# Neighbourhood attention steps regrouped on TensorE: scores, both heads' transposes, values

## The chip, the cores and the metric

The kernel is one launch on one core of a Trainium2 chip. The metric is the device time of that launch in microseconds; lower is better. A core has five engines that matter here: TensorE (PE, with its weight loads shown as PEld), VectorE (DVE), ScalarE (ACT), GpSimd (POOL) and SyncE (SP, which here issues loads). They run on their own and wait for each other by semaphores.

## What is computed

Two blocks in a row over 1024 positions of width 1024. The first block is two layers; each normalises, projects, runs three kinds of attention (latent, neighbourhood, differential), gates and projects back. The second block is a state space mixer, another attention and two wide feed-forward parts, and takes most of the time. The change touches neighbourhood attention alone, whose core in the reference is:

```python
def neighborhood_attention(q, k, v, rpb, scale):       # 16 rows of 64 columns, 6 heads of 64
    ...
    def one(r):
        r0 = jnp.clip(r - kr // 2, 0, rows - kr)
        q_r = lax.dynamic_index_in_dim(qg, r, axis=1, keepdims=False)
        k_r = lax.dynamic_slice_in_dim(kg, r0, kr, axis=1)[:, :, col_idx]
        v_r = lax.dynamic_slice_in_dim(vg, r0, kr, axis=1)[:, :, col_idx]
        ...
        s = jnp.einsum('bchd,brcjhd->bhcrj', q_r, k_r, preferred_element_type=jnp.float32) * scale
        s = s + bias.transpose(0, 2, 1, 3)[None].astype(jnp.float32)
        p = jax.nn.softmax(s.reshape(B, H, GRID_W, kr * kc), axis=-1).reshape(B, H, GRID_W, kr, kc)
        return jnp.einsum('bhcrj,brcjhd->bchd', p.astype(v.dtype), v_r)
```

## The kernel before

Each layer has a projection stage, then this neighbourhood stage, then a differential and a latent stage. Between stages every engine drains and waits for the other three (`phase_end`), and TensorE runs a few filler products (`keep_busy`) so as not to stand idle.

The neighbourhood stage is 24 steps: 3 pairs of heads (hp) times 8 tiles of 128 queries (t). Step s handles both heads of a pair, units u = 2s and 2s + 1. A query tile sees a window of keys: 512 of them in an outer step (t = 0, 1, 6, 7) and 576 in an inner one (t = 2 to 5, `inner` true), of which 12 exist per layer. The data passes through four engines:

- TensorE `scores(s)` (L1412): both heads' scores, one head in each half of the array's rows, into PSUM banks 0 to 3. It waits until the maxima of the step before are taken (m_ready 2s).
- VectorE `top(u)` (L3151 to L3167): one fused custom operation adds the bias and takes the maximum (L3161), and a small operation negates it (L3166), which raises m_ready. Each third of the stage needs its bias: top(0), top(16) and top(32) first wait for bias_in0 or bias_in1 (L3151).
- ScalarE `exps(u)` (L2247): the exponential with its sum (a second small record, the accumulator read).
- TensorE `probs_t(u)` (L1426): one head's probabilities are transposed in pieces of 128 keys into banks 4 and 5, four for an outer step and five (the last 64 wide) for an inner one.
- ScalarE `evacuate(u)` (L2257) copies the transposed tile to SBUF; for the odd head of an inner step VectorE copies the 64-key rest (`probs_t`, L3173).
- TensorE `values_of(s)` (L1442): the product with the values, both heads side by side in bank 6; an inner step has a last part over 64 rows.
- VectorE `out(s)` (L3178): the copy of the result.

TensorE's order in one pass of the loop is: probs_t(2s - 1), scores(s + 1), probs_t(2s), values_of(s - 1). The transposed buffers are three: one for the odd heads and two for the even.

After 8 steps, a pair's sums are inverted (L3209) and widened by GpSimd into a table that lies over the pair's bias in SBUF (`na_wides`, L623; the table of pair 0 over bias 0). In steps 11, 12, 19 and 20 TensorE transposes halves of such a table (`factors`, L1455, bank 7), and VectorE multiplies the outputs by it (`normed_out`, L3187). VectorE also does ten pieces of a key rotation in steps 10 to 19 (`key_rope`, L2936 to L2944).

The third pair's bias uses the same memory as the first pair's table. Its load is issued by SyncE, in code that the change leaves as it is:

```python
                sp.wait_ge(sems["t_done"], 6 * layer + 2)                                  # L888
                rows = a["na_bias"][layer * 3 + 2].rearrange("p (j n) -> p j n", j=2)
                sp.dma_start(na_bias[0], rows).then_inc(sems["bias_in0"], 16)              # L890
                for rr in range(2):
                    q, first = slice(64 * rr, 64 * rr + 64), (4 + rr) * GW
                    sp.dma_start(na_inner[2][q, :, rr * GW:rr * GW + NA_W], rows[q, :, first:first + NA_W])\
                        .then_inc(sems["bias_in0"], 16)                                    # L893
```

`t_done` rises by one with each factor turn (four in this stage, two in the next), so L888 waits for the second factor turn of the layer.

In the last pass TensorE also issues the first scores of the differential stage (`df_scores`, L1474), VectorE takes their maxima (`maximum`, L2928) and ScalarE the exponentials (`df_exp`, L2265).

## Time and profile before

| | us |
|---|---|
| median of 3 timed runs | 3862.62 |
| lowest of them | 3857.7 |
| the profiled execution | 3865.42 |
| its span, first to last instruction | 3863.6 |

The three timed runs were 3862.62, 3857.7 and one of 12884.99. The mean granted TensorE clock of the profiled execution is 0.995 of full speed. In the profile, "busy" is the time in which an engine has an instruction under way; "idle before" is what it stood before an instruction, with what released it. "issue" there means that no event of another engine is seen that released it.

### The profile page before, as it was taken

How to read it: one execution, taken by the hardware profiler on the slowest of the kernel's cores; microseconds unless marked ns; L12 is line 12 of the kernel's file. 1: busy time of each engine (PE TensorE's matmuls, PEld its weight loads, DVE VectorE, ACT ScalarE, POOL GpSimd, SP SyncE). 2: the span in 40 equal slices, each digit the busy share in tenths (PEclk: the TensorE clock that was granted, in tenths of full speed). 3: DMA queues.
4: the chain of work that ended last, by engine and by line, in shares of the span. 5: the costliest groups of instructions: out<-in, count | busy, mean ns of one | idle time of the engine just before them, and what ended most of it. 6: DMA issues, size and time to landing. Idle time of an engine off the chain costs nothing.

```text
span 3863.6 us, 53821 instructions
## 1 busy us (share of the span) xinstructions
PE 3774.8 (98%) x21662; PEld 2942.4 (76%) x21662; DVE 2660.7 (69%) x3327; ACT 1931.0 (50%) x2848; POOL 659.3 (17%) x747
## 2 busy tenths in 40 slices
PE   8999999999999999999999899999999999999999
PEld 5876667887876667887854668888888888888887
DVE  4446967675346967534445654989889869888898
ACT  5336866324336866324356444444445554444454
POOL 0120121001120121011059921000001430000010
PEclk9999999999999999999999999999999999999999
DMA  5232000453332000331100011111111111111111
GB/s 210 93 96 53 1 1 12 175 210 107 93 96 53 1 1 13 120 117 71 50 16 1 26 44 61 67 59 44 55 66 55 48 41 66 55 44 55 66 55 66
DMA packets 67735, 247.55 MB, mean 64 GB/s; under 512 B 15648, under 2 KB 16288, under 8 KB 55456
## 3 DMA queue, kind: packets, MB, share of 16 engines
q1 hardware_dynamic: 53648, 193.51, 14.9%
q10 hardware_dynamic: 13840, 50.60, 3.5%
q8 instruction: 173, 2.83, 0.3%
q14 instruction: 74, 0.61, 0.0%
HBM read 206.34 MB, written 29.36 MB: 61 GB/s over the span
## 4 chain that ended last, share of the span: by engine, by line
PE 82%; DVE 6%; POOL 4%; ACT 3%; issue 3%; DMA 1%; DVEq 0%; SPq 0%; ACTq 0%; POOLq 0%
PE ps L1786 31%; PE ps L1042 13%; PE ps L1294 3%; PE ps L1296 3%; PE ps L1295 3%; PE ps L1474 2%; PE ps L1157 2%; PE ps L1190 2%; PE ps L1532 2%; PE ps L1521 2%; PE ps L1426 2%; PE ps L1442 1%; PE ps L1412 1%; DMA w<-in_wstream 1%; PE ps L1175 1%
## 5 line engine op out<-in xcount | busy, mean ns | idle before, releaser
L1786 PE MATMUL ps<-x_piece1hi,w_piece1hi 128*128 128x512 f32 x672 | 262.4, 390 | 0.2 <-DVE x_piece1lo L3523 0.2
L1786 PE MATMUL ps<-x_piece0hi,w_piece0hi 128*128 128x512 f32 x672 | 262.3, 390 | 0.0
L1786 PE MATMUL ps<-x_piece0hi,w_piece0lo 128*128 128x512 f32 x672 | 261.5, 389 | 0.0
L1786 PE MATMUL ps<-x_piece1hi,w_piece1lo 128*128 128x512 f32 x672 | 261.4, 389 | 0.0
L1786 PE MATMUL ps<-x_piece0lo,w_piece0hi 128*128 128x512 f32 x672 | 261.4, 389 | 0.0
L1786 PE MATMUL ps<-x_piece1lo,w_piece1hi 128*128 128x512 f32 x672 | 261.4, 389 | 0.0
L1786 PE MATMUL ps<-x_piece2hi,w_piece2lo 128*128 128x512 f32 x672 | 261.4, 389 | 0.0
L1786 PE MATMUL ps<-x_piece2hi,w_piece2hi 128*128 128x512 f32 x672 | 261.4, 389 | 0.0
L1786 PE MATMUL ps<-x_piece2lo,w_piece2hi 128*128 128x512 f32 x672 | 261.4, 389 | 0.0
L1042 PE MATMUL ps<-n_hi_m,w_lo 128*128 128x512 f32 x576 | 225.5, 391 | 0.0
L4045 POOL TENSOR_TENSOR rope_cos<-rope_cos,arena 128x512 f32<-128x512 f32 x42 | 65.4, 1557 | 734.1 <-ACT arena L2497 731.0
L2928 DVE TENSOR_REDUCE small<-ps 128x1 f32<-128x1024 f32 x128 | 154.3, 1212 | 26.8 <-PE ps L1474 26.8
L2989 DVE TENSOR_REDUCE small<-ps 128x1 f32<-128x1024 f32 x96 | 113.0, 1219 | 79.6 <-PE ps L1164 79.4
L2265 ACT ACTIVATE h<-ps,small 128x1024 f32<-128x1024 f32 x128 | 142.6, 1114 | 46.8 <-DVE small L2928 46.7
L4045 POOL TENSOR_TENSOR rope_sin<-rope_sin,arena 128x512 f32<-128x512 f32 x28 | 45.2, 1615 | 640.7 <-ACT arena L2497 638.3
L2551 ACT ACTIVATE m<-m 128x1024 f32<-128x1024 f32 x80 | 85.0, 1062 | 132.5 <-DVE m L3567 104.0
L1786 PEld LDWEIGHTS ps<-x_piece1hi,w_piece1hi 128*128 128x128 f32 x672 | 126.1, 188 | 27.2 <-DVE x_piece1lo L3523 0.6
L1786 PEld LDWEIGHTS ps<-x_piece0lo,w_piece0hi 128*128 128x128 f32 x672 | 126.1, 188 | 26.6 <-issue 0.5
L1786 PEld LDWEIGHTS ps<-x_piece0hi,w_piece0hi 128*128 128x128 f32 x672 | 126.1, 188 | 26.6 <-DVE w_piece1lo L3516 0.2
L1786 PEld LDWEIGHTS ps<-x_piece1lo,w_piece1hi 128*128 128x128 f32 x672 | 126.1, 188 | 26.6 <-issue 0.5
L1786 PEld LDWEIGHTS ps<-x_piece1hi,w_piece1lo 128*128 128x128 f32 x672 | 126.1, 188 | 26.3
L1786 PEld LDWEIGHTS ps<-x_piece0hi,w_piece0lo 128*128 128x128 f32 x672 | 126.1, 188 | 26.2
(514 smaller groups left out, 10722.2 us busy)
## 6 DMA issues: line engine op xcount, KB each, us to landing
w<-in_wstream SPq DMA_DIRECT2D x87, 1024.0 KB, 5.1
arena<-in_wstream SPq DMA_DIRECT2D x40, 1024.0 KB, 4.9
arena<-in_wstream ACTq DMA_DIRECT2D x16, 1024.0 KB, 5.1
n_saved<-n_hi_m SPq DMA_DIRECT2D x16, 512.0 KB, 7.3
n_saved<-n_lo SPq DMA_DIRECT2D x16, 512.0 KB, 8.3
n_hi_h<-n_saved SPq DMA_DIRECT2D x16, 512.0 KB, 8.0
n_lo<-n_saved SPq DMA_DIRECT2D x16, 512.0 KB, 9.0
out<-h ACTq DMA_DIRECT2D x32, 256.0 KB, 2.2
```

Source lines behind the costliest of these rows:

```text
L1042: last = mm(dst, a_part[:, k, wcols], b_part[:, tile0 + k, :], start=(k == 0 and b_part is hi and a_part is wb[0]), stop=(k == nk - 1 and ...
L1157: mm(ps[:, 2 * j + hf, :], lt_split(hp, 0, q, r)[a_part], lt_split(hp, 1, keys, r)[b_part], start=(part == 0), stop=False)
L1190: last = mm(ps[64 * j:64 * j + 64, 6, 0:P], lt_v[:, b, hp * P + 64 * j:hp * P + 64 * j + 64], lt_pt_of(2 * s + j)[:, b * P:b * P + P], sta ...
L1294: mm(dst, wb[0][:, k, wcols], hi[:, k, :], start=(step == 0), stop=False)
L1295: mm(dst, wb[0][:, k, wcols], lo[:, k, :], start=False, stop=False)
L1296: last = mm(dst, wb[1][:, k, wcols], hi[:, k, :], start=False, stop=(step == KT - 1))
L1786: last = mm(dst[:, e, :], a_part[:, pair, k, f], b_part[:, k, :], start=(n in FRESH and half == 0 and k == 0 and t == 0), stop=(half == 1 ...
L2265: nc.scalar.activation(df_p[:, 2 * (c % 3) + i, :], psf[:, 2 * i * HALF:(2 * i + 2) * HALF], ACT.Exp, bias=negm[:, e:e + 1], accum_out=sum ...
L2551: nc.scalar.activation(x, x, ACT.Square if st.kind == "up" else ACT.Sigmoid).then_inc(sems["unit_done"], 1)
L2928: V.reduce_max(negm[:, u:u + 1], src, AX.X, negate=True).then_inc(sems["m_ready"], 1)
L2989: V.reduce_max(negm[:, u:u + 1], psf[:, 2 * j * HALF:(2 * j + 2) * HALF], AX.X, negate=True)\
L4045: G.tensor_tensor(out=x, in0=x, in1=ring[:, r % 2, :], op=ALU.add).then_inc(sems["t_added"], 1)
```

## The change

- TensorE's order in a pass becomes scores(s + 1), probs_t(s), values_of(s - 1). probs_t now takes a step: both heads' transposes in one group. In an inner step the two 64-key rests come first, into bank 5; then four transposes of the even head into bank 4 and four of the odd head into bank 7. t_full rises once for each head.
- Evacuation is by head: ScalarE copies the even head (bank 4) and, in inner steps, both rests; VectorE copies the odd head (bank 7). pt_act and pt_dve now count steps.
- The transposed buffers become two pairs, by the parity of the step; the fourth buffer is new (`na_pt_odd`).
- `top` multiplies by -1.0 and takes a minimum, so the negated maximum comes from the fused operation itself; the exponential takes scale -1.0, and L3166 goes.
- The factor turns go to bank 5 and to steps 14, 15, 22 and 23 (`NA_FACTORS_AT`), after values_of; an inner turn of the next pair that would reuse bank 5 waits for their multiplication.
- The first differential scores and their maxima come one pass earlier, in step 23. At the start the eight filler products stand between scores(1) and the first transposes.

```diff
-NA_INNER_AT = [sum(x[3] for x in NA_PAIRS[:s]) for s in range(NA_STEPS + 1)]
+NA_FACTORS_AT = {NT * (hp + 1) + NT - 2 + hf: (hp, hf) for hp in range(NA_H // 2 - 1) for hf in range(2)}
...
         def na_pt_of(u):
-            return na_pt[:, 1, :] if u % 2 else na_odd[:, 0, :] if u // 2 % 2 else na_pt[:, 0, :]
+            if u // 2 % 2:
+                return na_pt_odd if u % 2 else na_odd[:, 0, :]
+            return na_pt[:, u % 2, :]
...
-                    def probs_t(u):
-                        pe.wait_ge(sems["exp_done"], T.since("exp_done", u + 1))
-                        if u:
-                            pe.wait_ge(sems["pt_act"], T.since("pt_act", u))
-                        if u and u % 2 == 0:
-                            pe.wait_ge(sems["pt_dve"], T.since("pt_dve", NA_INNER_AT[u // 2]))
-                        for b, size in key_tiles(NA_PAIRS[u // 2][3]):
-                            last = nc.tensor.transpose(ps[0:size, 4 + b // 4, (b % 4) * P:(b % 4) * P + P],
-                                                       na_p_of(u)[:, b * P:b * P + size], ident)
-                        last.then_inc(sems["t_full"], 1)
+                    def probs_t(s):
+                        hp, t, _, inner = NA_PAIRS[s]
+                        pe.wait_ge(sems["exp_done"], T.since("exp_done", 2 * s + 2))
+                        if s:
+                            pe.wait_ge(sems["pt_act"], T.since("pt_act", s))
+                        if inner and s - 3 in NA_FACTORS_AT:
+                            pe.wait_ge(sems["na_m_done"], T.since("na_m_done", 2 * hp - 2))
+                        for j in range(2 if inner else 0):
+                            nc.tensor.transpose(ps[0:GW, 5, j * P:j * P + P], na_p_of(2 * s + j)[:, NA_W:NA_INNER], ident)
+                        for j in range(2):
+                            if s and j:
+                                pe.wait_ge(sems["pt_dve"], T.since("pt_dve", s))
+                            for b in range(NA_W // P):
+                                last = nc.tensor.transpose(ps[:, 7 if j else 4, b * P:b * P + P],
+                                                           na_p_of(2 * s + j)[:, b * P:b * P + P], ident)
+                            last.then_inc(sems["t_full"], 1)
...
                     for s in range(NA_STEPS + 1):
-                        if s == NA_STEPS:
+                        if s + 1 < NA_STEPS:
+                            scores(s + 1)
+                        elif s + 1 == NA_STEPS:
                             pe.wait_ge(sems["m_ready"], T.since("m_ready", NA_U))
...
                                 df_scores(0, i)
-                        if s:
-                            probs_t(2 * s - 1)
-                        if s + 1 < NA_STEPS:
-                            scores(s + 1)
-                        if s < NA_STEPS:
-                            probs_t(2 * s)
                         if s == 0:
                             keep_busy(7, 8)
+                        if s < NA_STEPS:
+                            probs_t(s)
                         if s:
                             values_of(s - 1)
-                        if s > NT and s % NT in (3, 4):
-                            factors(s // NT - 1, s % NT - 3)
+                        if s in NA_FACTORS_AT:
+                            factors(*NA_FACTORS_AT[s])
...
-                    def evacuate(u):
-                        act.wait_ge(sems["t_full"], T.since("t_full", u + 1))
-                        if u == 2:
+                    def evacuate(s):
+                        act.wait_ge(sems["t_full"], T.since("t_full", 2 * s + 1))
+                        if s == 1:
                             act.wait_ge(sems["restored"], 2 * 16 * KT * (layer + 1))
-                        if u >= 3:
-                            act.wait_ge(sems["o_full"], T.since("o_full", u // 2 - 1 + u % 2))
-                        width = NA_K if u % 2 == 0 and NA_PAIRS[u // 2][3] else NA_W
-                        nc.scalar.activation(na_pt_of(u)[:, 0:width], psf[:, 4 * HALF:4 * HALF + width], ACT.Copy)\
-                            .then_inc(sems["pt_act"], 1)
+                        if s >= 2:
+                            act.wait_ge(sems["o_full"], T.since("o_full", s - 1))
+                        for j in range(2 if NA_PAIRS[s][3] else 0):
+                            nc.scalar.activation(na_pt_of(2 * s + j)[0:GW, NA_W:NA_K], ps[0:GW, 5, j * P:j * P + P], ACT.Copy)
+                        nc.scalar.activation(na_pt_of(2 * s)[:, 0:NA_W], ps[:, 4, :], ACT.Copy).then_inc(sems["pt_act"], 1)
...
-                    for s in range(NA_STEPS + 1):
-                        if s < NA_STEPS:
-                            exps(2 * s)
-                        if s:
-                            evacuate(2 * s - 1)
-                        if s < NA_STEPS:
-                            exps(2 * s + 1)
-                            evacuate(2 * s)
+                    exps(0)
+                    exps(1)
+                    for s in range(NA_STEPS):
+                        evacuate(s)
+                        if s + 1 < NA_STEPS:
+                            exps(2 * s + 2)
+                            exps(2 * s + 3)
...
-                            na_inner[hp][:, j, :] if inner else na_bias[hp % 2][:, j, e * GW:e * GW + NA_W], 1.0, 4 * MASKED, ALU.add, ALU.max, mx[:, u:u + 1])\
-                            .then_inc(sems["v_link"], 1)
-                        dve.wait_ge(sems["v_link"], T.next("v_link"))
-                        V.tensor_scalar(negm[:, u:u + 1], mx[:, u:u + 1], -1.0, None, ALU.mult)\
+                            na_inner[hp][:, j, :] if inner else na_bias[hp % 2][:, j, e * GW:e * GW + NA_W], -1.0, -4 * MASKED, ALU.add, ALU.min, negm[:, u:u + 1])\
                             .then_inc(sems["m_ready"], 1)
-                    def probs_t(u):
-                        dve.wait_ge(sems["t_full"], T.since("t_full", u + 1))
-                        if u >= 3:
-                            dve.wait_ge(sems["o_full"], T.since("o_full", u // 2 - 1 + u % 2))
-                        V.tensor_copy(na_pt_of(u)[0:GW, NA_W:NA_K], ps[0:GW, 5, 0:NA_K - NA_W]).then_inc(sems["pt_dve"], 1)
+                    def probs_t(s):
+                        dve.wait_ge(sems["t_full"], T.since("t_full", 2 * s + 2))
+                        if s >= 2:
+                            dve.wait_ge(sems["o_full"], T.since("o_full", s - 1))
+                        V.tensor_copy(na_pt_of(2 * s + 1)[:, 0:NA_W], ps[:, 7, :]).then_inc(sems["pt_dve"], 1)
...
                     for s in range(NA_STEPS + 1):
-                        if s == NA_STEPS:
-                            maximum(0, psf[:, 0:2 * HALF], NA_STEPS)
-                        if s and NA_PAIRS[s - 1][3]:
-                            probs_t(2 * s - 1)
-                        if s == NA_STEPS:
-                            maximum(1, psf[:, 2 * HALF:4 * HALF], NA_STEPS)
                         if s + 1 < NA_STEPS:
                             top(2 * s + 2)
                             top(2 * s + 3)
+                        elif s + 1 == NA_STEPS:
+                            for i in range(2):
+                                maximum(i, psf[:, 2 * i * HALF:2 * i * HALF + 2 * HALF], NA_STEPS)
+                        if s < NA_STEPS:
+                            probs_t(s)
                         if s:
                             out(s - 1)
...
-                        if s > NT and s % NT in (3, 4):
-                            normed_out(s // NT - 1, s % NT - 3)
+                        if s in NA_FACTORS_AT:
+                            normed_out(*NA_FACTORS_AT[s])
```

## Rows read from the trace of the kernel before

**Rows 1.** The page: busy time and share of the span by engine

```profile
PE 3774.8 (98%) x21662; PEld 2942.4 (76%) x21662; DVE 2660.7 (69%) x3327; ACT 1931.0 (50%) x2848; POOL 659.3 (17%) x747
```

**Rows 2.** By stretch: length, busy PE, PEld, DVE, ACT, POOL, granted clock, DMA share, GB/s

```profile
265.00:363.50 98.50, 96.30 (x849) 63.68 (x849) 62.38 (x202) 69.51 (x152) 16.63 (x15) 1.00 0.20 57
...
277.00:353.00 76.00, 75.73 (x691) 50.13 (x692) 51.87 (x171) 55.47 (x123) 5.39 (x4) 1.00 0.16 44
```

**Rows 3.** Waits, 275 to 358 us: who for whom, us, times, longest

```profile
PEld ps L1426 <- issue: 12.0, 30, 1.0
...
PEld ps L1412 <- DVE small L3166: 0.7, 4, 0.2
```

**Rows 4.** Timeline (start us, length us), TensorE's weight loads, one inner step

```profile
280.62 0.30 PEld L1412 LDWEIGHTS ps<-arena 64*128 64x128 f32 x4 [0.20 <-issue]
...
281.85 0.50 PEld L1426 LDWEIGHTS ps<-mats,m 128*128 128x128 f32 x5
282.54 0.85 PEld L1442 LDWEIGHTS ps<-h,arena 128*64 128x64 f32 x16 [0.20 <-issue]
...
284.63 0.30 PEld L1412 LDWEIGHTS ps<-arena 64*128 64x128 f32 x4 [0.20 <-issue]
```

**Rows 5.** Timeline, TensorE's products, an outer turn and outer values

```profile
303.84 0.66 PE L1426 MATMUL ps<-mats,m 128*128 128x128 f32 x4
304.43 1.09 PE L1442 MATMUL ps<-h,arena 128*64 128x128 f32 x16
305.45 0.66 PE L1426 MATMUL ps<-mats,m 128*128 128x128 f32 x4
```

**Rows 6.** Timeline, weight loads, a factor turn directly ahead of a turn

```profile
312.99 0.42 PEld L1455 LDWEIGHTS ps<-mats,h 128*128 128x128 f32 x4 [0.17 <-issue]
313.38 0.55 PEld L1426 LDWEIGHTS ps<-mats,m 128*128 128x128 f32 x5
314.12 0.30 PEld L1412 LDWEIGHTS ps<-arena 64*128 64x128 f32 x4 [0.20 <-issue]
```

**Rows 7.** Timeline, ScalarE: an evacuation and an exponential

```profile
280.73 0.60 ACT L2257 ACTIVATE h<-ps 128x512 f32<-128x512 f32 x1 [0.26 <-PE ps L1426]
281.22 0.77 ACT L2247 ACTIVATE m<-m,small 128x576 f32<-128x576 f32 x1
281.89 0.19 ACT L2247 ACTIVATION_READ_ACCUMULATOR m<-m,small 128x1 f32 x1
```

**Rows 8.** Timeline, VectorE's narrow copy

```profile
280.73 0.28 DVE L3173 COPY h<-ps 64x128 f32<-64x128 f32 x1 [0.34 <-PE ps L1426]
```

**Rows 9.** Timeline, VectorE's top(32): the fused operation and its accumulator read

```profile
327.75 0.69 DVE L3161 CUSTOM_DVE_ANT_0 h<-ps,h 128x512 f32<-128x512 f32 x1 [0.96 <-PE ps L1412]
328.37 0.08 DVE L3161 DVE_READ_ACCUMULATOR2_ANT small<- 128x1 f32 x1
```

**Rows 10.** Timelines of VectorE, ScalarE and TensorE at the end of the stage

```profile
359.75 2.35 DVE L2928 TENSOR_REDUCE small<-ps 128x1 f32<-128x1024 f32 x2 [0.59 <-PE ps L1474]
...
363.15 0.19 ACT L2265 ACTIVATION_READ_ACCUMULATOR h<-ps,small 128x1 f32 x1
...
363.49 0.18 PEld L1474 LDWEIGHTS ps<-df_hi 32*128 32x128 f32 x1 [0.45 <-ACT h L2265]
```

**Rows 11.** Timelines of TensorE and load queue; the queue's issues (size, us to landing)

```profile
317.54 0.66 PE L1455 MATMUL ps<-mats,h 128*128 128x128 f32 x4
...
318.23 0.34 SPq L890 DMA_DIRECT2D h<-in_na_bias  x1
318.61 1.22 SPq L893 DMA_DIRECT2D w<-in_na_bias  x2
...
w<-in_na_bias SPq DMA_DIRECT2D x2, 256.0 KB, 6.6
```

**Rows 12.** By stretch, the next stage (columns as in rows 2)

```profile
368.00:371.20 3.20, 0.78 (x7) 0.48 (x6) 3.20 (x3) 1.20 (x2) 0.00 (x0) 1.00 1.04 247
371.20:385.00 13.80, 13.80 (x78) 10.26 (x76) 9.86 (x12) 9.91 (x15) 1.02 (x3) 0.51 0.61 125
```

More of the change, by code:

```diff
@@ L1402, in _ @@
                 phase_end(LAYER_COUNTS.n % 4, 5)
-                with T.span(s_full=NA_STEPS, m_ready=NA_U, exp_done=NA_U, t_full=NA_U, pt_act=NA_U, pt_dve=NA_INNER_AT[-1], o_full=NA_STEPS,
+                with T.span(s_full=NA_STEPS, m_ready=NA_U, exp_done=NA_U, t_full=NA_U, pt_act=NA_STEPS, pt_dve=NA_STEPS, o_full=NA_STEPS,
                             o_free=NA_STEPS, t_done=4, na_m_done=4):
@@ L1417, in key_tiles @@
                         return [(b, P) for b in range(NA_W // P)] + [(NA_W // P, GW)] * inner
-                    def probs_t(u):
-                        pe.wait_ge(sems["exp_done"], T.since("exp_done", u + 1))
-                        if u:
-                            pe.wait_ge(sems["pt_act"], T.since("pt_act", u))
-                        if u and u % 2 == 0:
-                            pe.wait_ge(sems["pt_dve"], T.since("pt_dve", NA_INNER_AT[u // 2]))
-                        for b, size in key_tiles(NA_PAIRS[u // 2][3]):
-                            last = nc.tensor.transpose(ps[0:size, 4 + b // 4, (b % 4) * P:(b % 4) * P + P],
-                                                       na_p_of(u)[:, b * P:b * P + size], ident)
-                        last.then_inc(sems["t_full"], 1)
+                    def probs_t(s):
[14 more added lines that the diff above has]
+                            last.then_inc(sems["t_full"], 1)
                     def values_of(s):
                         hp, t, s0, inner = NA_PAIRS[s]
-                        pe.wait_ge(sems["pt_act"], T.since("pt_act", 2 * s + 2))
-                        pe.wait_ge(sems["pt_dve"], T.since("pt_dve", NA_INNER_AT[s + 1]))
+                        pe.wait_ge(sems["pt_act"], T.since("pt_act", s + 1))
+                        pe.wait_ge(sems["pt_dve"], T.since("pt_dve", s + 1))
                         if s:
@@ L1450, in factors @@
                             pe.wait_ge(sems["na_m_done"], T.since("na_m_done", 2 * hp + hf))
-                        factor_turns(hp, hf, 7)
+                        factor_turns(hp, hf, 5)
                     def factor_turns(hp, hf, bank):
@@ L2237, in _ @@
                 inner_bias(layer, 1, "bias_in1")
-                with T.span(s_full=NA_STEPS, m_ready=NA_U, exp_done=NA_U, t_full=NA_U, pt_act=NA_U, pt_dve=NA_INNER_AT[-1], o_full=NA_STEPS,
+                with T.span(s_full=NA_STEPS, m_ready=NA_U, exp_done=NA_U, t_full=NA_U, pt_act=NA_STEPS, pt_dve=NA_STEPS, o_full=NA_STEPS,
                             o_free=NA_STEPS, t_done=4, na_m_done=4):
@@ L3144, in _ @@
                 phase_end()
-                with T.span(s_full=NA_STEPS, m_ready=NA_U, exp_done=NA_U, t_full=NA_U, pt_act=NA_U, pt_dve=NA_INNER_AT[-1], o_full=NA_STEPS,
+                with T.span(s_full=NA_STEPS, m_ready=NA_U, exp_done=NA_U, t_full=NA_U, pt_act=NA_STEPS, pt_dve=NA_STEPS, o_full=NA_STEPS,
                             o_free=NA_STEPS, t_done=4, na_m_done=4):
@@ L3182, in normed_out @@
                         dve.wait_ge(sems["o_free"], T.since("o_free", NT * (hp + 1)))
-                        out_times(hp, hf, 7)
+                        out_times(hp, hf, 5)
                     def out_times(hp, hf, bank):
```

4 lines of the change are left out of this document (3 added, 1 removed).

## The prediction

> **What bounds the kernel now.** The page comes first: TensorE is busy for 98% of the span [rows 1], mostly on lines of other stages. The edited stage runs once per layer and lasts 98.5 us in the first [rows 2], so some 197 us of 3863.6 for both: whatever happens here moves the whole by tenths of a per cent unless a step breaks. About 2% (77 us) is what a measurement of this kernel tells from no change, and I give my chances by that.
>
> Next, who waits inside the stage. In the 76 us of steady stepping TensorE is busy 75.7 us at the full granted clock (2.4 GHz) [rows 2]. In the list of waits its weight loads wait for "issue", and for another engine next to never: 0.7 us in all for the negated maximum [rows 3]. So the stage goes at TensorE's own pace, and what it pays besides its columns is a gap of some 0.2 us whenever one kind of product follows another. The timeline of one inner step (576 keys) shows it: scores at 280.62, a turn of five transposes from 281.85 to the values at 282.54, then the values and the other head's turn, and scores again at 284.63, 4.01 us later [rows 4]. A turn of five costs 0.69 us from start to start; in outer steps (512 keys) a turn of four costs 0.59 (303.84 to 304.43) and the values 1.02 (304.43 to 305.45) [rows 5].
>
> **The merge of the two turns.** The kernel before holds its own measurement of a merge. At 312.99 four factor transposes stand directly ahead of a turn of five, and the nine end at the scores of 314.12: 1.13 us [rows 6]. Apart they would take 0.59 and 0.69 [rows 4, 5], 1.28. The waits between them (the turn waits on three counts) cost nothing, so a merge saves 0.15 us. One more full transpose is 0.10 to 0.11; ten in one group are then 1.24 instead of 1.39, eight 1.02 instead of 1.17. Steps 2 to 22, 21 of them, give 21 x 0.15 = 3.15 us per layer.
>
> In the new turn the narrow transposes (64 columns) come first, then the full ones. In the turn of five the narrow one follows four full ones and adds only 0.10 us (0.69 against 0.59) [rows 4, 5], so I cost that order at nothing. The Trainium skill, TensorEngine Tiling, section Key Properties, says that changing the tiling mode drains the engine. If narrow and full transposes were two modes, each inner step would pay one change back, an estimate of 12 x 0.15 = 1.8 us per layer; the row shows no such change.
>
> **The four factor turns** lose a part of it. Before they lean on a transpose turn and cost 1.13 - 0.69 = 0.44 us each; after, in steps 14, 15, 22 and 23, they stand between values and scores as a group of their own, 0.59. 4 x 0.15 = 0.6 us lost per layer.
>
> **ScalarE and VectorE, costed at nothing, and by what cover.** ScalarE now has per inner step two narrow copies, one 512 copy and two exponentials, all between one turn and the next. A 512 copy lets the next operation start 0.50 us after it; an exponential ends with its accumulator read 0.86 after its start [rows 7]. For a 64x128 copy on ScalarE there is no row: more than nothing, less than those 0.50; I take the 0.28 of VectorE's copy of that shape [rows 8]. From the start of a turn of ten: 0.91 to the end of its first half, 0.56, 0.50, 0.77 for the first exponential, 0.86 for the second, 0.05 to TensorE: 3.65 us, 3.1 to 4.1 by the bounds. The new period is 4.01 - 0.15 = 3.86. It fits; where it does not, 12 inner steps lose the excess. VectorE loses a negation and takes a 128x512 copy (nearest row: the 0.69 of the fused operation on 512 columns [rows 9]) for its narrow one: 0.8 + 0.8 + 0.7 + 0.3 = 2.6 us per step and up to 0.7 of key rotation, under 3.86. The fused minimum has no row either; it reads and writes what the maximum does, so I take the same 0.69; a third more would still be covered. The removed negation was not on the path [rows 3].
>
> **Start and end.** At the start the second turn waits some 0.5 us for ScalarE, as both exponentials now stand ahead of it, and the group that is gone gives about as much back: an estimated 0.06 us lost. At the end the first differential scores come one pass earlier. The two maxima (2.35 us) then stand ahead of VectorE's last copy, and the last values, waiting for it, come about when they did. But ScalarE's two large exponentials, which were the last thing before the next stage (their read at 363.15 ends 363.34, TensorE follows at 363.49 [rows 10]), are over by then, and VectorE's last reciprocal closes the stage an estimated 0.75 us sooner. Per layer: 3.15 - 0.6 - 0.06 + 0.75 = 3.2 us gained, 6.5 for both.
>
> **What the moved factor turn releases.** The second factor turn does more than feed VectorE: L888 makes the load queue wait for it (t_done at 6*layer + 2) before it loads the third pair's bias. In the trace the turn runs 317.54 to 318.20 and the queue issues at 318.23; the last of its three loads is issued about 1.0 us later and lands 6.6 us after that [rows 11]. So the bias is whole some 7.6 us after the turn. Before, the turn is in step 12 and the bias is first needed by top(32), in step 15, which runs at 327.75, 9.5 us after the issue, and waits for the scores [rows 9]: the load is covered, with 2 us to spare. After, the turn is the last thing that TensorE does in step 15, and top(32) stands first in VectorE's step 15. The cover is gone altogether.
>
> Queued behind top(32) on VectorE are top(33), the copy of the odd head, the output of step 14, the factor multiplication and a key rotation. ScalarE's next exponential waits for top(32); TensorE goes on to the end of the factor turn and stops, since scores(17) need top(33). The load queue has nothing else due. From the turn's end: 7.65 us to the landing, 0.05 to VectorE, 0.8 + 0.75 for the two tops, 0.15 to TensorE = 9.4 us, where the scores would have started at once. The factor turn needs nothing of top(32), so it is a stall and no deadlock. Afterwards VectorE works its queue off and is late for top(34); some 0.5 us of that reaches TensorE.
>
> **Sum.** Per layer 9.4 + 3 - 3.2 = +9.2 us, for both +18.4. The profiled span of 3863.6 becomes 3882. That execution took 3865.42 with what lies around its span, 2.8 over the median of 3862.62; the median should become 3862.62 + 18.4 = 3881.
>
> **Rivals.**
> 1. The bias is there in time, and the kernel is faster than before. For it I find only an error of mine in the order of the steps; against it the queue's issue 0.03 us after the very turn that moves. It decides from a landing before the end of scores(16). 3862.6 - 6.5 = 3856. Chance 0.05.
> 2. The stall as above, but the merge saves nothing: narrow and full transposes drain between them, or ScalarE's chain is at its upper bound (4.1 over 3.86, 12 steps, 2.9 us). At most the 3.15 us of both layers come back: 3887. Chance 0.15.
> 3. Slower by more than 2%: the half clock, once there, stays for the rest of the stage. Steps 17 to 23, about 25 us, would take twice that: 2 x (9.4 + 25 - 3.2) = 62, 3925. It passes 77 us only if 7.5 us more are lost in each next stage. For it: 13.8 us at half clock with TensorE busy [rows 12]; against it: 76 us of the same steps at the full one [rows 2]. Chance 0.03, of which a third over 2%.
>
> **How the numbers follow.** The forecast has 0.77. Its own range comes from the clock: with no loss 2 x (9.9 - 3.2) = 13, 3876; with all of it 2 x (9.4 + 6.9 - 3.2) = 26, 3889. Scatter between executions (3857.7 to 3865.4 before) and rival 2 widen this to 3868 to 3894, which leaves out rivals 1 and 3 and the tails. Within 2% is 3785 to 3940; chances are 0.01 faster, 0.97 within, 0.02 slower.
>
> **What the profile after would show.** One group of eight or ten transposes of 1.02 or 1.24 us per step: the merge. The bias load issued at the end of a factor turn near 328 us, and VectorE idle some 10 us ahead of the fused operation of top(32), released by a load: the stall. A granted clock of 0.5 in a stretch behind it: the clock's part. If TensorE waits for ScalarE in inner steps, that cover was misjudged; if no engine is idle around step 15, the forecast is wrong and rival 1 right.

## The result and the profile after

| | before | after |
|---|---|---|
| median, us | 3862.68 (6 runs) | 3875.06 (6 runs) |
| range of them | 3857.7 to 12884.99 | 3872.04 to 3881.64 |
| the profiled execution | 3865.42 | 3881.47 |
| its span | 3863.6 | 3879.7 |

The kernel became slower by a third of a per cent: the ratio of after to before is 1.0031, with an interval of 1.0021 to 1.0041. The interval leaves out 1, so the rise is clear of the scatter; by the 2% bound of the prediction it counts as no change. The median rose by 12.4 us where 18.4 were forecast, and 3875 lies inside the range given. The ratios here and below are formed without the executions in a disturbed, slow state (the one of 12884.99 and, in the first experiment, one of 3987.44), which the medians and the numbers of runs include.

The page's busy times (busy us, share of the span, instructions):

```profile
PE 3771.7 (97%) x21662; PEld 2946.6 (76%) x21662; DVE 2668.3 (69%) x3255; ACT 1908.9 (49%) x2848; POOL 661.8 (17%) x747
```

Against [rows 1] TensorE has the same 21662 instructions and 3 us less busy time, in a span 16 us longer: it stood idle for more. VectorE has lost 72 instructions net (96 negations and 24 narrow copies gone, 48 wide copies new); ScalarE's number is unchanged. The stretches of the stage say where the idleness is. The columns are length, busy PE, PEld, DVE, ACT and POOL, granted clock, DMA share and GB/s; the first two lines are the stage in both layers, then its steady part, the stall, and two stretches at half clock:

```profile
265.50:370.40 104.90, 94.68 (x849) 65.39 (x848) 65.71 (x166) 57.99 (x152) 17.11 (x16) 0.95 0.19 54
1141.40:1247.00 105.60, 95.26 (x849) 65.83 (x848) 65.71 (x166) 58.00 (x152) 17.08 (x15) 0.95 0.19 53
277.00:327.00 50.00, 50.00 (x482) 34.67 (x480) 33.89 (x88) 32.28 (x88) 4.83 (x4) 1.00 0.14 35
327.00:337.00 10.00, 0.99 (x12) 0.58 (x8) 1.45 (x5) 0.72 (x2) 0.00 (x0) 0.67 0.55 170
330.30:340.60 10.30, 3.69 (x12) 2.07 (x12) 4.42 (x12) 2.05 (x6) 0.00 (x0) 0.50 0.40 135
1212.70:1217.80 5.10, 5.05 (x24) 3.22 (x26) 3.79 (x9) 2.83 (x9) 0.00 (x0) 0.50 0.00 0
```

From the first scores of the stage to the first of the next, the stage took 98.31 us before and takes 104.72 now (265.71 to 370.43); in the second layer it went from 98.3 to 105.5. That is 6.4 + 7.2 = 13.6 us for both, against 12.4 in the medians. The other 2.5 us of the two spans' difference lie outside this stage: 0.5 of them before it begins, the rest behind it, where the two traces have stretches of 3.4 us at half clock in different places (at 514 and 2258 us before, at 879 and 1398 after). No run here explains these. The half clock of the next stage, too, differs between kernels whose code there is the same (13.7 us in each layer before, 3.4 and 13.6 in the first experiment, in one profiled execution of each). The medians carry all of that; the stage's own length does not, and is the safer measure in what follows.

The stall is one place per layer. TensorE's products there (start, length, engine, line, operation, output and inputs, shapes, count, idle before and releaser):

```profile
326.22 1.09 PE L1452 MATMUL ps<-h,arena 128*64 128x128 f32 x16
327.24 0.66 PE L1465 MATMUL ps<-mats,h 128*128 128x128 f32 x4
336.91 2.08 PE L1416 MATMUL ps<-arena 64*128 64x512 f32 x4 [9.01 <-DVE small L3168]
338.92 1.86 PE L1436 MATMUL ps<-mats,h 128*128 128x128 f32 x8
...
341.74 1.30 PE L1416 MATMUL ps<-arena 64*128 64x512 f32 x8
```

The load queue and VectorE in the same stretch, in the same columns:

```profile
327.93 0.34 SPq L894 DMA_DIRECT2D h<-in_na_bias  x1
328.31 1.23 SPq L897 DMA_DIRECT2D w<-in_na_bias  x2
...
324.85 0.68 DVE L2951 TENSOR_TENSOR arena<-arena,h 128x512 f32<-128x512 f32 x1
335.55 0.69 DVE L3168 CUSTOM_DVE_ANT_0 h<-ps,h 128x512 f32<-128x512 f32 x1 [10.02 <-DMA w<-in_na_bias]
```

Read them together. The factor turn (L1465) starts at 327.24. The queue, which had waited for it, issues the bias at 327.93 where before it issued at 318.23 [rows 11]. VectorE has nothing that it may do from 325.53 to 335.55, when the last part of the load releases top(32). TensorE's scores(17) (336.91) wait for top(33). Then the first scores take 2.08 us for what took 1.13 before: that is the half clock.

And the inner step, by TensorE's weight loads:

```profile
281.01 0.30 PEld L1416 LDWEIGHTS ps<-arena 64*128 64x128 f32 x4 [0.17 <-issue]
...
282.23 0.14 PEld L1431 LDWEIGHTS ps<-mats,m 128*64 128x64 f32 x2
282.37 0.91 PEld L1436 LDWEIGHTS ps<-mats,m 128*128 128x128 f32 x8
283.45 0.85 PEld L1452 LDWEIGHTS ps<-h,arena 128*64 128x64 f32 x16 [0.17 <-issue]
284.47 0.20 PEld L1452 LDWEIGHTS ps<-h,arena 64*64 64x64 f32 x4 [0.17 <-issue]
284.84 0.30 PEld L1416 LDWEIGHTS ps<-arena 64*128 64x128 f32 x4 [0.17 <-issue]
```

Scores to scores is 3.83 us (281.01 to 284.84), where [rows 4] had 4.01. The narrow transposes run 282.23 to 282.37 and the full ones follow without a gap. The group of ten takes 1.22 us to the values. All of TensorE's 50 us in 277 to 327 are busy.

The account of the first layer, in differences between the starts of scores (scores(23) is the last; "next" is the first of the next stage):

| stretch | before | after | difference |
|---|---|---|---|
| first scores to scores(3) | 11.77 | 11.83 | +0.06 |
| scores(3) to scores(16) | 49.39 | 46.59 | -2.80 |
| scores(16) to scores(17), the stall | 3.25 | 12.78 | +9.53 |
| scores(17) to scores(18), half clock | 3.26 | 4.83 | +1.57 |
| scores(18) to scores(23) | 19.86 | 18.06 | -1.80 |
| scores(23) to next | 10.78 | 10.63 | -0.15 |
| sum | 98.31 | 104.72 | +6.41 |

So the regrouping does what it should, and the moved factor turn takes back more than that. The runs below take the pieces apart.

### The profile page after: what moved, and what is told of

Same layout as the page of the kernel before. It is cut to its first block, busy times and chain, and to the rows that moved or that the text cites. A ratio compares the mean times of both kernels' runs of the same rounds, so it can differ in the third digit from the quotient of the medians.

```text
span 3879.7 us, 53675 instructions
## 1 busy us (share of the span) xinstructions
PE 3771.7 (97%) x21662; PEld 2946.6 (76%) x21662; DVE 2668.3 (69%) x3255; ACT 1908.9 (49%) x2848; POOL 661.8 (17%) x747
## 4 chain that ended last, share of the span: by engine, by line
PE 56%; DVE 5%; POOL 3%; ACT 2%; issue 2%; DVEq 0%; ACTq 0%; POOLq 0%
PE ps L1794 31%; PE ps L1046 4%; PE ps L1298 2%; PE ps L1299 1%; PE ps L1300 1%; PE ps L1484 1%; PE ps L1584 1%; PE ps L1161 1%; PE ps L1194 1%; PE ps L1540 1%; PE ps L1529 1%; PE ps L1736 1%; PE ps L1734 1%; PE ps L1735 1%; PE ps L1752 1%
```

## The experiments

**The load's dependency removed, all else kept.** The theory: the loss is entirely the bias load that waits for the moved factor turn. So give it a reason to come early. The third pair's bias could not be loaded because the first pair's table lay in its memory; here that table goes to memory that is free in the stage, and the load waits only for the first pair's sums to be inverted, at which its scores no longer need bias 0.

```diff
+        na_wide0 = [region(w[hf], 2 * NA_INNER, NT // 2, P)[0] for hf in range(2)]
...
-                sp.wait_ge(sems["t_done"], 6 * layer + 2)
+                sp.wait_ge(sems["lat_rs"], 2 * LAT_PAIRS * layer + 1)
...
+                            wide = na_wides[hp][:, 4 * hf + i, :] if hp else na_wide0[hf][:, i, :]
+                            last = nc.tensor.transpose(ps[:, bank, i * P:i * P + P], wide, ident)
...
```

The part left out has GpSimd write the table's two halves to the new place.

> The changed kernel, with the first pair's table put into free columns of w[0] and w[1] instead of over bias 0, so that the load of the third pair's bias no longer waits for the second factor turn; it waits for the first pair's reciprocal (step 8). Factor turns stay in steps 14, 15, 22, 23. If the late load causes the stall, the 9.0 and 9.1 us idle stretches ahead of scores(17) and the half clock behind them are gone: from scores(16) to scores(18) the changed kernel takes 17.6 us against 6.8 without a stall, so 2 x 10.8 = 21.6 us less than 3875.1, 3853.5 us, 9 us under the kernel before. Rival: the stall is only part and the regrouping itself gains nothing; then it cannot come under 3862.7 us. Rival: the idle stretch has another cause (bank 5, the multiplication); then 3875 stays.

Measured: 3854.33 us (11 runs), ratio 0.9978 (0.9969 to 0.9987). The queue, VectorE's top(32) and TensorE around the place where the stall was:

```profile
302.43 0.34 SPq L895 DMA_DIRECT2D h<-in_na_bias  x1
...
325.38 0.69 DVE L3170 CUSTOM_DVE_ANT_0 h<-ps,h 128x512 f32<-128x512 f32 x1
...
323.95 1.13 PE L1417 MATMUL ps<-arena 64*128 64x512 f32 x4
...
327.64 1.13 PE L1417 MATMUL ps<-arena 64*128 64x512 f32 x4
...
330.75 1.30 PE L1417 MATMUL ps<-arena 64*128 64x512 f32 x8
```

The load goes out 25 us earlier, top(32) no longer waits for it, and the steps are 3.69 and 3.11 us where after had 12.78 and 4.83. The stage takes 93.93 us, 10.8 less than in after and 4.4 less than before; over two layers the latter is 8.8. The median is 8.7 us under that of before in the same set of runs (3862.99). The theory holds, and the regrouping is worth 4.4 us per layer, more than the 3.2 forecast.

**The factor turns alone moved in the kernel before.** The other direction: if the moved turn makes the loss, it makes it without any regrouping.

```diff
-                        if s > NT and s % NT in (3, 4):
-                            factors(s // NT - 1, s % NT - 3)
+                        if s in NA_FACTORS_AT:
+                            factors(*NA_FACTORS_AT[s])
...
```

VectorE's multiplication by the factors moves in the same way.

> The kernel before, with one part of the change alone: the factor turns and their multiplications in steps 14, 15, 22, 23 instead of 11, 12, 19, 20. If the place of the second factor turn makes the stall, it appears here too: about 9 us idle and 1.5 to 2.5 us of slow clock per layer, some 21 us in all, 3883 us. If the stall needs the new grouping (the third bank, the copies by head), this stays at 3862.7 us within 1 us.

Measured: 3888.51 us (5 runs), ratio 1.0065 (1.0053 to 1.0077). Around the stall, TensorE:

```profile
327.77 0.66 PE L1456 MATMUL ps<-mats,h 128*128 128x128 f32 x4
...
337.89 2.08 PE L1413 MATMUL ps<-arena 64*128 64x512 f32 x4 [9.03 <-DVE small L3167]
```

The same 9.0 us (9.28 in the second layer) with the old groups. The stage is 109.6 us long, 11.3 more than before. Two layers of that are 22.6 us, of the 25.5 by which the median lies over before's (3862.99), so some 3 us lie outside this stage. Inside it, the half clock lasted into the steps after the stall: scores(17) to scores(18) take 5.71 and 5.51 us, where before has 3.26. In the next stage, whose code is untouched, the half clock takes 13.65 + 3.41 us, where before has 13.7; what the additional stretch cost was not measured, and why it came stays open.

**The fused minimum alone in the kernel before.**

```diff
-                            na_inner[hp][:, j, :] if inner else na_bias[hp % 2][:, j, e * GW:e * GW + NA_W], 1.0, 4 * MASKED, ALU.add, ALU.max, mx[:, u:u + 1])\
-                            .then_inc(sems["v_link"], 1)
-                        dve.wait_ge(sems["v_link"], T.next("v_link"))
-                        V.tensor_scalar(negm[:, u:u + 1], mx[:, u:u + 1], -1.0, None, ALU.mult)\
+                            na_inner[hp][:, j, :] if inner else na_bias[hp % 2][:, j, e * GW:e * GW + NA_W], -1.0, -4 * MASKED, ALU.add, ALU.min, negm[:, u:u + 1])\
...
```

> The kernel before, with the negated maximum from the fused minimum alone (96 negations of 0.15 us gone, exponential with scale -1). My prediction: nothing on the path, 3862.7 us within 1.5 us. Rival: the steps with a factor turn and a key rotation, where VectorE was late by 0.2 to 0.3 us, shorten: at most 8 such steps and 0.25 us, 3861.

The exponential's scale of -1.0 is in the part left out. Measured: 3863.90 us (12 runs), ratio 1.0004 (0.9994 to 1.0013): nothing, as forecast. It saves 0.3 us once per layer, at the stage's start (the stage takes 97.99 us, not 98.31), which is below what the runs tell apart. It served a second question. In the kernel before, the steps with factor turns are longer than the transposes in them explain, and a late VectorE was a suspect. Its weight loads of three scores in a row:

```profile
308.15 0.30 PEld L1412 LDWEIGHTS ps<-arena 64*128 64x128 f32 x4 [0.20 <-issue]
...
312.60 0.30 PEld L1412 LDWEIGHTS ps<-arena 64*128 64x128 f32 x4 [0.20 <-issue]
...
317.15 0.30 PEld L1412 LDWEIGHTS ps<-arena 64*128 64x128 f32 x4 [0.20 <-issue]
```

4.45 and 4.55 us, as before (4.44 and 4.55), against 4.01 unburdened. So the excess isn't the negation's. The trace of before shows where it comes from. TensorE may not start the next transposes until VectorE has copied the 64-key rest of the odd head (the wait on pt_dve), and in these steps that copy stands behind the factor multiplication and a piece of the key rotation. VectorE's copy and TensorE's weight loads there, after scores(14):

```profile
319.56 0.28 DVE L3173 COPY h<-ps 64x128 f32<-64x128 f32 x1
...
318.67 0.30 PEld L1412 LDWEIGHTS ps<-arena 64*128 64x128 f32 x4 [0.20 <-issue]
319.96 0.50 PEld L1426 LDWEIGHTS ps<-mats,m 128*128 128x128 f32 x5 [0.98 <-issue]
```

The copy ends at 319.84 and the transposes begin at 319.96, 1.29 us after the scores, where an unburdened outer step has 1.06. The list of waits names the copy as what released them. After scores(13) the same copy costs 0.10. In the kernel with the fused minimum alone the copy ends at 318.32 and the transposes begin at 318.44: it is as late there, since what stands ahead of it starts with the factor turn and not with the negation. A late VectorE was the cause after all, by its queue and not by the negation.

**TensorE kept busy through the stall.** The half clock was forecast as 3 us of the loss per layer. Here after gets fifty filler products behind the factor turn, so that TensorE waits for the same load but is not idle.

```diff
+                        if s == 2 * NT - 1:
+                            pe.wait_ge(sems["pt_act"], T.since("pt_act", s + 1))
+                            keep_busy(4, 50)
```

> The changed kernel, with 50 filler products (about 8.2 us) on TensorE behind the second factor turn of each layer, within the idle stretch. The stall's length stays, since it is set by the load. If the slower steps after it are due to the clock, the granted clock stays at full there, scores(17) to scores(18) take 3.1 us instead of 4.8 and 5.5, and the time falls by 2 to 5 us, to 3871. If they are due to VectorE's queue alone, the time stays at 3875.

Measured: 3871.07 us (11 runs), ratio 1.0023 (1.0015 to 1.0032). TensorE:

```profile
326.21 0.66 PE L1465 MATMUL ps<-mats,h 128*128 128x128 f32 x4
326.62 8.94 PE L1010 MATMUL ps<-mats_r 128*128 128x384 f32 x50
336.20 1.13 PE L1416 MATMUL ps<-arena 64*128 64x512 f32 x4 [0.63 <-DVE small L3171]
```

The stretch behind the stall (columns as in the first view by stretch):

```profile
336.00:342.00 6.00, 5.80 (x52) 3.97 (x54) 5.93 (x18) 3.95 (x11) 1.04 (x1) 1.00 0.00 0
```

The stall did not get shorter: scores(16) to scores(17) is 13.10 us in the first layer and 13.32 in the second, where after had 12.78 and 12.90. The load took 0.3 to 0.4 us longer here, 7.9 and 8.15 us from its first issue to top(32), against 7.6 and 7.7. But the scores behind it take 1.13 us again and the next step 3.14. The clock was at its upper level there. That step is 0.03 longer than the 3.11 of the kernel without a stall, so VectorE's queue, for which the forecast had 0.5 us inside its clock term, costs nothing. What the half clock takes in after is the rest: 4.83 - 3.11 = 1.7 us in the first layer, 5.46 - 3.11 = 2.35 in the second. Of these 4.1 us for both layers, the longer load takes 0.7 back: the stage is 1.3 and 1.9 us shorter than in after, 3.2 together. The medians are 4.0 apart, which their scatter does not tell from 3.2.

**Top(32) waits for its own part of the load only.** The load is three transfers; top(32) and the three after it read only the first, of 1152 KB. Here the two others count on another semaphore, waited for two steps later.

```diff
-                        .then_inc(sems["bias_in0"], 16)
+                        .then_inc(sems["bias_in1"], 16)
...
-                            dve.wait_ge(sems[f"bias_in{hp % 2}"], T.next(f"bias_in{hp % 2}", 48 if hp else 16))
+                            dve.wait_ge(sems[f"bias_in{hp % 2}"], T.next(f"bias_in{hp % 2}", 48 if hp == 1 else 16))
+                        if u == 36:
+                            dve.wait_ge(sems["bias_in1"], T.next("bias_in1", 32))
```

> The changed kernel, with top(32) waiting only for the first of the three late loads (1152 KB); the two loads for the inner steps are waited for at top(36). In the changed kernel the first was issued at 327.93 and took 5.5 us, the last was there when top(32) started at 335.55. If the length of the stall is that of the loads, it shortens by 335.5 - 333.4 = 2.1 us per layer, and the time falls by 4.2 us, to 3871. Rival: the first load takes its time from sharing the DMA engines with the other two and top(36) stalls instead; then 3875 stays.

Measured: 3872.85 us (7 runs), ratio 1.0028 (1.0018 to 1.0039). VectorE at top(32) and TensorE behind it:

```profile
332.31 0.69 DVE L3170 CUSTOM_DVE_ANT_0 h<-ps,h 128x512 f32<-128x512 f32 x1 [7.85 <-DMA h<-in_na_bias]
...
333.68 2.08 PE L1416 MATMUL ps<-arena 64*128 64x512 f32 x4 [6.85 <-DVE small L3170]
```

The half-clock stretch:

```profile
331.20:338.00 6.80, 4.33 (x16) 2.49 (x18) 4.72 (x13) 2.69 (x7) 0.00 (x0) 0.50 0.31 78
```

The releaser is now the first transfer, and the idle time fell by what was forecast for it, 9.01 to 6.85 and 9.13 to 6.88. In the second layer the whole stage gained as much, 2.2 us. In the first it gained 1.9: TensorE resumed 2.5 us into a half-clock stretch of 6.8, so that 4.4 us of it fell on work, against 3.6 in after; in the second layer it was 5.1 against 5.0. The shorter stall did not shorten the clock's part. The rival is out: the first load took 5.45 us from its issue beside the two others, and top(36) stalls nobody, since scores(18) to scores(19) take 3.28 us as in after (3.27). The medians are 2.2 us apart where the two stages give 4.1, and their intervals overlap; the reading rests on the traces.

**The turn split again.** This run isolates the merge. It is the kernel without the stall (the first experiment), but with the values between the two heads' transposes, which makes four groups per step again; the narrow ones stay with the even head.

```diff
-                            probs_t(s)
+                            probs_t(s, (0,))
                         if s:
                             values_of(s - 1)
+                        if s < NA_STEPS:
+                            probs_t(s, (1,))
```

> As e1_table_moved, with the step's transposes cut in two again: even head, values of the step before, odd head (factor turn directly behind it), scores. That is one change of kind more per step, with the same products and the same waits. If the gap at each change of kind is what the regrouping saves, the steps go from 3.83 to 4.0 us (inner) and from 3.10 to 3.26 (outer): 24 x 0.16 = 3.8 us per layer, less 0.6 for the factor turns, 6.5 us in all, 3861 us. If the saving came from the removed negation and the split copies, it stays at 3854.

Measured: 3861.24 us (11 runs), ratio 0.9995 (0.9986 to 1.0004). One inner step in its weight loads:

```profile
284.70 0.30 PEld L1417 LDWEIGHTS ps<-arena 64*128 64x128 f32 x4 [0.17 <-issue]
...
288.09 0.42 PEld L1437 LDWEIGHTS ps<-mats,h 128*128 128x128 f32 x4 [0.17 <-issue]
288.68 0.30 PEld L1417 LDWEIGHTS ps<-arena 64*128 64x128 f32 x4 [0.17 <-issue]
```

and the same step in the kernel with one turn:

```profile
284.65 0.30 PEld L1417 LDWEIGHTS ps<-arena 64*128 64x128 f32 x4 [0.17 <-issue]
...
288.48 0.30 PEld L1417 LDWEIGHTS ps<-arena 64*128 64x128 f32 x4 [0.17 <-issue]
```

3.98 us with four groups, 3.83 with three, same instructions. The stage is 2.9 us longer (96.82), 5.8 for both layers; the median is 6.9 higher. The merge is worth 0.15 us a step here; the remaining 0.03 of the 4.01 before is not taken apart. Over the stage 21 x 0.15 would be 3.15; the first two factor turns, which here stand directly behind the odd head's transposes, give 0.3 back (their steps take 4.06 and 3.69 us in both kernels).

**The factor turn directly ahead of the transposes.** Based on the kernel without the stall. A factor turn that stands between values and scores is a group of its own; ahead of the transposes it joins theirs.

```diff
+                        if s in NA_FACTORS_AT:
+                            pe.wait_ge(sems["pt_act"], T.since("pt_act", s))
+                            factors(*NA_FACTORS_AT[s])
                         if s < NA_STEPS:
                             probs_t(s)
                         if s:
                             values_of(s - 1)
-                        if s in NA_FACTORS_AT:
-                            factors(*NA_FACTORS_AT[s])
```

> As e1_table_moved, with each factor turn directly ahead of the step's transposes (one kind of product) instead of between values and scores. A factor turn then costs 0.44 us instead of 0.59: 4 x 0.15 = 0.6 us per layer, 1.2 in all, 3853 us. In the trace the steps with a factor turn show it, the time itself hardly can. Rival: the turn's place is free, because those steps wait for VectorE's multiplication and key rotation; then steps 14 and 15 are as long as in e1_table_moved (4.06 us for 15 to 16).

Measured: 3854.55 us (11 runs), ratio 0.9981 (0.9972 to 0.9990), the same as without the edit (3854.33). TensorE:

```profile
319.20 1.13 PE L1417 MATMUL ps<-arena 64*128 64x512 f32 x4
320.26 0.66 PE L1467 MATMUL ps<-mats,w 128*128 128x128 f32 x4
...
323.11 1.13 PE L1417 MATMUL ps<-arena 64*128 64x512 f32 x4
...
326.72 1.13 PE L1417 MATMUL ps<-arena 64*128 64x512 f32 x4
```

The two steps take 3.91 and 3.61 us, against 4.06 and 3.69: 0.23 per pair of turns, not 0.30, and 0.4 us for the whole stage (93.53). In the median that is lost in the scatter.

**No fillers at the end.** The trace of after showed something that the forecast had passed over. The end of the stage there, VectorE and TensorE:

```profile
369.50 0.24 DVE L3212 RECIPROCAL small<-small 128x16 f32<-128x16 f32 x1
...
369.36 1.13 PE L1010 MATMUL ps<-mats_r 128*128 128x384 f32 x5
370.43 0.49 PE L1484 MATMUL ps<-df_hi 32*128 32x512 f32 x1
```

The stage's last work, the reciprocal, is over at 369.74, but TensorE goes through five filler products until 370.43. Before, they lay in the shadow of ScalarE's exponential [rows 10]. This run takes them out of the previous one.

```diff
-                phase_end(4, 5)
+                phase_end(4, 0)
```

> As e5_factors_ahead, without the five filler products at the end of the stage. They follow the last values and end 1.07 us later, past VectorE's last reciprocal, so the next stage's scores wait for them: 0.5 us sooner per layer without them, 1 us in all, 3852 us. Rival: without them the granted clock falls earlier in the next stage, where it was half for 3 to 14 us in all runs, and 2 to 6 us are lost.

Measured: 3851.72 us (7 runs), ratio 0.9971 (0.9961 to 0.9982), the lowest of all kernels here. The end:

```profile
358.19 0.24 DVE L3215 RECIPROCAL small<-small 128x16 f32<-128x16 f32 x1
...
358.59 0.18 PEld L1486 LDWEIGHTS ps<-df_hi 32*128 32x128 f32 x1 [0.89 <-issue]
```

The next stage begins 0.16 us after the reciprocal's end, and the stage takes 93.06 us, 0.47 less. The medians differ by 2.8 us; the traces account for about 1 of them in this stage, and the intervals overlap. The rival did not show: the half clock of the next stage lasts 10.2 and 6.8 us here, not longer than the 13.7 and 13.6 of the previous run. (The 3 to 14 us named there for all runs were 17 in the one with the factor turns alone.)

## Why the prediction was right, and where not

**The stall: right.** The order of events is the one forecast: load queue behind the moved turn, issue near 328 (327.93), top(32) released by a load after some 10 us (10.02), TensorE behind top(33). It was put at 9.4 us over an unstalled step. In after it is 12.78 - 3.69 = 9.1, with the 3.69 from the kernel without a stall. The landing took 7.6 us from the first issue (327.93 to 335.55), and 7.65 from the turn's end, as the sum had it. What was put too high are the two tops, which take 0.61 us each from start to start (335.55, 336.16, 336.77), not 0.8 and 0.75. With TensorE kept busy the stall is 9.4, but there the landing took 0.3 longer; that this is the forecast number is chance. The two kernels that touch only this, one way and the other, confirm it as the cause. Rival 1, the bias in time, is out.

**The half clock: right in kind, the size 1.5 times too large.** Forecast 3 us per layer, between 0 and 6.9; measured 1.7 and 2.35. The view by stretch shows why. The clock's lower level began 2.4 us into the stall of the first layer (at 330.31) and 3.9 into that of the second (at 1207.54), and lasted 10.24 us in both, so the larger part of it fell into the idle time: 3.6 and 5.0 us of it were left for work, of which half is lost. The prediction took 3 as a share of the 13.8 us that [rows 12] show in the next stage, which was a guess between its bounds. The 0.5 for VectorE's queue in it were nothing. The Trainium skill, TensorE: Matmul & The Clock Gate, Part 1, says that an idle TensorE is gated down and sustained activity restores it. Of that the stall agrees with the first half, in after and in the run with the fillers (0.50 behind the idle stall, 1.00 behind the busy one). For the second half the rows are mixed: behind the stall the clock came back with TensorE at work, but in [rows 12] it stays at half for 13.8 us with TensorE busy throughout. Rival 3, the half clock for the rest of the stage, is out.

**The merge: right, a little too small.** 0.15 us a step was forecast; four groups against three with the same instructions gives 0.15, and the whole step from before to after 0.18 in inner and 0.15 to 0.16 in outer steps. Rival 2, in which narrow and full transposes drain between them, is out: 282.23 to 282.37 to 283.45 leaves no room for it. The Trainium skill, TensorEngine Tiling (Array Packing), Key Properties, has a change of tiling mode drain the engine. The gaps of 0.17 us at the changes from transposes to values and from values to scores fit that, though no run here shows that they are a drain; between 64 and 128 columns of weights there is none, so these behave here as one mode.

**ScalarE's chain: right that it is covered.** Its narrow copies, whose price had no row, in after (same columns):

```profile
283.12 0.27 ACT L2265 ACTIVATE m<-ps 64x128 f32<-64x128 f32 x1 [1.04 <-PE ps L1436]
283.29 0.26 ACT L2265 ACTIVATE arena<-ps 64x128 f32<-64x128 f32 x1
283.45 0.58 ACT L2266 ACTIVATE m<-ps 128x512 f32<-128x512 f32 x1
```

0.27 us as taken, but the next one starts 0.17 after it, so the pair costs 0.33 rather than 0.56. The list of waits names ScalarE ahead of some transposes, up to 0.8 us; these waits cost nothing, since the products themselves leave no idle time in the 50 us from 277 to 327.

**The factor turns: this step failed.** The prediction had 0.6 us per layer lost, 0.15 for each, by pricing them before at 0.44 from [rows 6]. That row gives the transposes right; the steps around them say more. Before, scores(12) to (13), (13) to (14) and (14) to (15) took 4.44, 4.55 and 4.07 us, 0.43 + 0.54 + 0.23 = 1.2 over the unburdened steps, not 0.88. After, two turns cost what they were put at, 0.59 each: 4.06 and 3.69 in the kernel without the stall, where the same two steps of the first pair, without factor turns, take 3.48 and 3.10. So moving them lost nothing for the first pair (1.18 for 1.20). For the second, what is left of the -1.80 in the account above after five merges at 0.17 is 0.95 removed, where the forecast had 0.88. The steps, not the group, were the right measure: an excess over the neighbours' period holds what the instructions' own time does not. The extra 0.3 is TensorE waiting for VectorE's copy of the 64-key rest, 0.10 us after scores(13) and 0.23 after scores(14), as read above from the trace of before. The prediction took the waits of these steps as free. In after ScalarE makes that copy, and the steps with a factor turn are longer by no more than the turn's own 0.59.

**The end: a term with two errors.** The forecast for scores(23) to the next stage was 10.78 - 0.15 (merge) + 1.18 (two factor turns) - 0.75 (end) = 11.06; measured is 10.63. Overlooked were the five fillers, which hold up the next stage by some 0.5 us (0.47 without them). Overlooked on the other side was that the last factor turn, at 366.83, runs while VectorE is still busy with the maxima and what is queued behind them, and TensorE waits 0.67 us more after it, so that turn costs nothing. The 0.3 that these leave (11.06 + 0.47 - 0.59 = 10.94, against 10.63) are not assigned.

**The start: the number right by luck.** +0.06 forecast, +0.06 measured. But the prediction had the removed negation off the path, and at the start it is on it: with the fused minimum alone, first scores to scores(3) take 11.44 us, not 11.77. So the regrouping costs 0.4 there (11.83 against 11.44), and the negation gives 0.33 back.

Put together, per layer: the regrouping gave 4.4 us where 3.2 were forecast (factor turns and merge some 0.7 better, the end 0.4), the stall took 9.1 rather than 9.4, and the clock about 2 rather than 3. All three errors go the same way, so none hides another. The net is 6.4 and 7.2 instead of 9.2, and the median rose by 12.4 instead of 18.4.

## What to carry to other kernels

A step that is moved takes with it every semaphore that it raises, those that another engine or a load queue counts on among them: before moving one, list who waits for its count, with the time from release to first use. Here a transfer had 2 us of slack and the move took it 9.7 us later, which turned a regrouping worth 4.4 us per layer into a loss of 6.4 to 7.2; moving a buffer so that the load no longer depends on the step kept the gain (3854.33, and 3851.72 with two details more). To price a step before moving it, take the excess of its period over its neighbours', beside its own instructions: here it held 0.3 us of waiting for another engine's queue.

## What the runs showed of the chip

- On TensorE a change between these kinds of products costs 0.15 us from start to start with nothing waited for: 3.98 against 3.83 us for four and three groups of the same instructions.
- The granted clock fell to its lower level 2.4 and 3.9 us after TensorE went idle in after and came back after 10.24 us in both layers; in the kernel with the shorter stall it fell after 4.4 and 5.1 us and held 6.83 us, of which 4.4 and 5.1 fell on work. What the engine did while it was low was to stand idle first and to work without a break then. The time at half clock that remains after a resumption did not shrink with the stall (3.6 and 5.0 us after 9 us idle, 4.4 and 5.1 after 6.9).
- A bias load of 1152 KB and two parts of 256 KB was whole 7.6 to 8.15 us after its first issue, and its first part, where it was waited for alone, was there after 5.45 and 5.49.
